# A bound on the experts' gather and scatter, with padding rows numbered past it

## The reference

```python
experts = (g_idx * EXPERTS_PER_GROUP + e_i).astype(jnp.int32)   # two of each token
...
pad_tok = jnp.full((p_len,), t, jnp.int32).at[dest].set(slot_tok[order])
pad_w = jnp.zeros((p_len,), jnp.float32).at[dest].set(slot_w[order])
...
hdn = jax.nn.silu(xb @ w1[e]) * (xb @ w3[e])
return hdn @ w2[e]
...
out = jnp.zeros((t + 1, dm), ys.dtype).at[pad_tok].add(ys * pad_w[:, None].astype(ys.dtype))
```

## Time and profile before

| | |
|---|---|
| median of three runs | 3437.43 us (3431.68 to 3441.14) |
| profiled execution, its own time | 3431.25 us |
| its span | 3429.7 us |
| mean granted TensorE clock | 0.932 of 2.4 GHz |
| PE, PEld, DVE, ACT, POOL busy | 84, 65, 45, 36, 9% of the span |
| DMA moved | 529.85 MB, mean 154 GB/s |
| the experts' phase | from about 1041 us to 1673 us |

### The profile page before, as it was taken

The page is one execution under the profiler, slowest core; times in us unless marked ns, Lnnn a source line. Parts: engine busy times, 40 slices in busy tenths (PEclk is TensorE's granted clock), DMA queues, the critical chain, the costliest instruction groups (busy, mean ns, idle before and its releaser), DMA issues. The chain is left out here.

```text
span 3429.7 us, 61238 instructions
## 1 busy us (share of the span) xinstructions
PE 2895.4 (84%) x22510; PEld 2246.3 (65%) x22510; DVE 1540.9 (45%) x2906; ACT 1219.3 (36%) x2193; POOL 301.7 (9%) x461
## 2 busy tenths in 40 slices
PE   7997885787977999999587999878887999868876
PEld 6785664565746887777476888744476888754455
DVE  3861666776251222222335411268744421068853
ACT  4332554566131000000333222268723222158831
POOL 0001641000021222221100000000000000000000
PEclk9998898898998999999798999979988999989988
DMA  5114553211358999999645221431054221251034
GB/s 184 68 70 145 142 151 99 72 35 44 115 189 309 375 379 380 379 376 378 234 132 172 90 103 49 135 119 38 10 175 163 95 98 73 98 172 31 14 123 166
DMA packets 241534, 529.85 MB, mean 154 GB/s; under 512 B 27760, under 2 KB 110640, under 8 KB 216720
## 3 DMA queue, kind: packets, MB, share of 16 engines
q1 hardware_dynamic: 216192, 464.40, 37.7%
q0 software_dynamic: 24080, 63.77, 6.6%
q10 hardware_dynamic: 1152, 0.27, 0.0%
HBM read 425.15 MB, written 104.15 MB: 154 GB/s over the span
## 5 line engine op out<-in xcount | busy, mean ns | idle before, releaser
L461 PE MATMUL ps<-in_wh,in_xh 128*128 (+1 forms) x1024 | 401.2, 392 | 0.0
L462 PE MATMUL ps<-in_wl,in_xh 128*128 (+1 forms) x1024 | 399.8, 390 | 0.0
L463 PE MATMUL ps<-in_wh,in_xl 128*128 (+1 forms) x1024 | 399.6, 390 | 0.0
L463 PEld LDWEIGHTS ps<-in_wh,in_xl 128*128 128x128 f32 x1024 | 193.0, 189 | 40.6
L461 PEld LDWEIGHTS ps<-in_wh,in_xh 128*128 128x128 f32 x1024 | 193.2, 189 | 39.7
L462 PEld LDWEIGHTS ps<-in_wl,in_xh 128*128 128x128 f32 x1024 | 193.1, 189 | 39.6
L1060 DVE TENSOR_TENSOR ex_hid<-ps,ex_act 32x128 f32<-32x128 f32 x96 | 28.2, 294 | 311.1 <-PE ps L1111 310.3
L461 PE MATMUL ps<-mix_in_wh,mix_in_xh 128*128 (+1 forms) x384 | 151.9, 396 | 9.0 <-DVE mix_in_out L381 5.5
L462 PE MATMUL ps<-mix_in_wl,mix_in_xh 128*128 (+1 forms) x384 | 149.9, 390 | 0.0
L463 PE MATMUL ps<-mix_in_wh,mix_in_xl 128*128 (+1 forms) x384 | 149.7, 390 | 0.0
L245 ACT COPY in_out<-ps 128x512 f32<-128x512 f32 x64 | 37.5, 587 | 248.7 <-PE ps L463 248.7
(11 more groups left out here) (412 smaller groups left out, 7281.2 us busy)
## 6 DMA issues: line engine op xcount, KB each, us to landing
ex_w_w1a<-in_w_dram SPq DMA_DIRECT2D x32, 1024.0 KB, 14.6
ex_w_w1b<-in_w_dram SPq DMA_DIRECT2D x32, 1024.0 KB, 15.6
ex_w_w3a<-in_w_dram SPq DMA_DIRECT2D x32, 1024.0 KB
ex_w_w3b<-in_w_dram SPq DMA_DIRECT2D x32, 1024.0 KB, 15.5
ex_w_w2a<-in_w_dram SPq DMA_DIRECT2D x32, 1024.0 KB, 15.6
ex_w_w2b<-in_w_dram SPq DMA_DIRECT2D x32, 1024.0 KB, 15.6
proj<-in_out SPq DMA_DIRECT2D x128, 256.0 KB, 2.0
da_w_ada<-in_w_ada_dram SPq DMA_DIRECT2D x32, 768.0 KB, 4.2
```

The costliest lines, as they stand in the source:

```text
L461: pe.matmul(o, xh[:, kt, tok], wb[0], start=(kt == 0), stop=False)
L462: pe.matmul(o, xh[:, kt, tok], wb[1], start=False, stop=False)
L463: last = pe.matmul(o, xl[:, kt, tok], wb[0], start=False, stop=(kt == KT - 1))
```

## The change

Both indirect transfers get an upper bound of 1023 on the index (`bounds_check=SEQ - 1`), and an index above it is not an error (`oob_is_err=False`). The padding triples name row 1024 to gather instead of row 0; their rows to add into were 1024 to 1151 before and stay so. So all indices of padding rows are above the bound, and the transfers are told to leave these rows out. Since rows of `xg` that are never gathered into would hold what memory held, POOL fills `xg` with zeros once, after the first index and row lists are asked for and before the first gather, and waits for that (`cleared`).

```diff
@@ expert_phase
-        copied = s.sem("copied")
+        copied, cleared = s.sem("copied"), s.sem("cleared")
...
                 pool.indirect_dma_start(out=xg[:], out_offset=None, in_=k.xn[:, :],
-                                        in_offset=bass.IndirectOffsetOnAxis(ap=idx_own[:, 0:1], axis=0)).then_inc(gathered, 16)
+                                        in_offset=bass.IndirectOffsetOnAxis(ap=idx_own[:, 0:1], axis=0), bounds_check=SEQ - 1, oob_is_err=False).then_inc(gathered, 16)
...
                 pool.indirect_dma_start(out=h[:, :], out_offset=bass.IndirectOffsetOnAxis(ap=row_own[:, 1:2], axis=0),
-                                        in_=y[:], in_offset=None, compute_op=ALU.add).then_inc(stored, 16)
+                                        in_=y[:], in_offset=None, compute_op=ALU.add, bounds_check=SEQ - 1, oob_is_err=False).then_inc(stored, 16)
...
             load_idx(0)
             load_row(0)
+            pool.memset(xg[:], 0.0).then_inc(cleared, 1)
+            pool.wait_ge(cleared, 1)
             gather(0)
@@ shape_constants
-    spares = np.stack([np.zeros(spare, int), SEQ + np.arange(spare) % P, np.zeros(spare, int)], 1).reshape(P, SPARE, 3)
+    spares = np.stack([np.full(spare, SEQ), SEQ + np.arange(spare) % P, np.zeros(spare, int)], 1).reshape(P, SPARE, 3)
```

## The result

| | before | after |
|---|---|---|
| median of 20 runs | 3435.43 us | 3439.09 us |
| lowest and highest | 3427.59 to 3441.14 | 3431.95 to 3446.31 |
| ratio, 95% interval | | **1.0015** (1.0008 to 1.0022) |
| span of the profiled execution | 3429.7 us | 3444.8 us |

The change is a loss of 0.15%, 5 us by the ratio. It is inside the bound of 0.3% that the prediction calls no change, but twenty runs each tell it from nothing, and it has the other sign than the 1.6 us of gain that was forecast.

What follows compares the result with a forecast made beforehand. DMA engines were taken to bound the expert phase, PE next. Profiled 3431.25 - 1.6 us (last gather), other terms zero, gave 3429.7 us, or 3436 us from the timed median 3437.43; own range 3428 to 3444, 8 in 10 3408 to 3444.

Steps and rivals of the forecast that it cites:

- The bound: Expert phase: DMA engines limit first, PE next; faster DMA can give about 1.2 us of the 18.4 us block.
- How a transfer is laid on the engines: Gather and scatter: 96 rows lie six consecutive per engine, so dropping the last rows leaves engine 0 its six.
- Step 1: Gather and scatter: 2144 padding rows not moved; worth 0 to 1.09 us per block, lower end taken.
- the 33rd gather: Last gather, all padding: leaves every engine, saving half of one block's q0 work, 1.6 us.
- The packets: POOL's queue q0: dropped rows leave no packets, so near 21900 packets after the change.
- Step 2: POOL's descriptor making: the compare on each index lies beside PE, hidden by slack; zero.
- Step 3: POOL's one memset of `xg`: 0.88 us, hidden in the 4.19 us wait for the index list; zero.
- Signs in the profile: Expert phase: period stays 18.4 us, `w1b` wait near 0.8 us per block, share 1.02 to 0.96, rate near 364 GB/s.
- A: Gather and scatter: rows dealt evenly over engines or a shared limit; 25 us faster, 3412 us; chance 0.22.
- B: Gather and scatter: the bound does not drop packets, rows clamped or moved anyway; 3437 us; chance 0.08.
- C: POOL's descriptor making: slow compare makes the scatter the bound; 16 us slower, 3453 us; chance 0.06.
- the 0.04 for the unforeseen: Whole kernel: chance 0.04 for what was not thought of, split between faster and slower.

Runs made afterwards that it cites:

- the even run: Kernel before, with bounds and the gather and scatter indices of two in every six rows raised above them, 32 rows per block dropped: 3403.74 us, ratio 0.9909.
- nothing scattered: Kernel before, with bounds and all 96 scatter indices of each block raised above theirs, the gather's inside: 3404.54 us, ratio 0.9911.
- the last 32 rows of each block: Kernel before, with bounds and the gather and scatter indices of partitions 64 to 95 raised above them: 3443.48 us, ratio 1.0030.
- the scatter alone: The change's bound on the scatter only, padding still gathering row 0, against the kernel before: 3448.57 us, ratio 1.0044.
- the gather alone: The change's bound on the gather only, the scatter's padding rows moved as before, against the kernel before: 3438.97 us, ratio 1.0012.
- the run with the bound idle: The change with padding numbers inside the bound (gather row 0, scatter bound 1151), so every row moves, against the kernel before: 3434.28 us, ratio 1.0005.
- once the padding was dealt: The change with each block's slots spread over the engines in the router, against the kernel before: 3415.36 us (0.9945); with one operation fewer per list 3411.35 us (0.9933).
- the four uneven runs: Against the kernel before: the change 1.0015, its bound on gather only 1.0012, on scatter only 1.0044, and partitions 64 to 95 dropped 1.0030.
- the pairs built for it: Kernel before moving only 64 rows, plus an additional load per block on sixteen, then ten partitions: 1.0489 and 1.0421 (28 KB pieces), 1.0433 and 1.0350 (8 KB).
- the 8 KB runs: Kernel before moving only 64 rows, plus three 8 KB pieces per partition and block on sixteen, then ten partitions: 3581.56 and 3555.45 us.

## Why the prediction was wrong, point by point

**The bound.** Right: DMA first, PE close behind. The estimate that faster DMA can give at most 1.2 us a block before PE binds held: 18.39 - 17.49 = 0.90 us in the even run and 0.97 with nothing scattered, with PE busy all of the time in both. One reading of the rows was loose: the two queues' 18.9 us a block are not the period of 18.4. They are 102.2% of it, since packets overlap, and 500 us hold 27.2 periods and not 27.

**How a transfer is laid on the engines.** Right for the index lists: the trace of before has 864 packets of 72 bytes in the 500 us, six triples of 12 bytes each, 32 a block. Six consecutive rows to an engine fits gather and scatter too: dropping two rows of every six gained 0.9 us a block, dropping the last 32 gained nothing, and with row i on engine i mod 16 both would have taken two rows from every engine. The rule of the Trainium skill named in the prediction (DMA: Bandwidth & Descriptors, "Why a DMA increments its semaphore by 16 and not by 1") agrees with it as to the 16 shares: a third fewer rows paid only where every share of six became smaller.

**Step 1, rows not moved: the step that failed.** The prediction took as its lower end "nothing, if the most loaded engine keeps all its rows", and then 1.6 us of gain for the 33rd gather. Zero was not the lower end. Uneven dropping costs: 5 us in the change, 10 us with the last 32 rows of each block, 15 us with the scatter alone, 4 us with the gather alone. The term measured +5 us, not -1.6. What the runs showed in its place: q1's packets took 4.3% longer (0.307 against 0.294 us), 3.7 points of share against the 5.8 that q0 gave up, and the rest went to engines that stood idle, so that the period grew by 0.12 us. An end of a range that is a resource's "no relief" is not a bound below when the same change can slow the others. Whether the 33rd gather gave anything can't be told beside this. Its price, half of a block's q0 work, was not measured by any run: q0's share changes with what runs beside it.

**The packets.** Wrong: near 21900 packets were expected on q0, and 24080 stood there. A dropped row is a small packet. It did not matter for the time where the rows were spread.

**Step 2, the compare.** Right to leave it at nothing: 951 to 1029 ns for the gather, 1490 and 1489 for the scatter, and 1.0005 for the run with the bound idle. **Step 3, the fill**: 0.97 us for 0.88, covered.

**Signs in the profile.** The period was to stay at 18.4 and came to 18.51, within the 0.3 us; the rate was to fall to 364 GB/s and fell to 363; `w1b` was still waited for. But the share was to fall from 1.02 to 0.96 and fell to 1.00: the idle engines were there, 10.7% of the time, but q1's longer packets filled much of the room.

**The rivals.** A's mechanism is not in the change, but its price was good: 25 us off, against 19 to 23 measured once the padding was dealt. B was half true in the packets and false in the bytes. C did not happen: DVE's copy waits for PE 27 times of 27. The real loss was none of the three, and lay in the 0.04 for the unforeseen. That the time still fell into the stated range says little: a loss of 5 us is smaller than the spread of the runs from which that range was taken.

**What stays open** is why dropping rows on some engines lengthens the weights' packets on the whole. Shown is that it goes with uneven dropping (0.298 to 0.311 us in the four uneven runs; 0.292 to 0.298 where the dropped rows of both transfers were spread, so the two kinds touch at one end). Small packets in a row are an unlikely cause: with six of them on every engine, the weights' packets that meet no row took 0.318 us. In the uneven runs themselves they were not tried apart. Not shown is that engines that run ahead of each other are the cause: the pairs built for it failed, and the run with nothing scattered has long packets without imbalance.

## What to carry to other kernels

Here rows saved in one piece at the end of a tile saved no time (1.0015 and 1.0030), and the same number taken evenly did (0.9909): spread the padding over the groups of consecutive partitions that each engine serves, and only then drop it. Before giving such a saving a lower bound of zero, ask what the relieved engines will do to the rest. Read the shares of both queues together with their packet counts, and then PE's waits and the period: a rising time per packet goes with a loss in the uneven runs, but with none where nothing was scattered.

## What was not expected of the hardware

- An index above the bound leaves a packet under 512 bytes: 2144 more of them for 2144 dropped rows, at the same total of 241534. Spread evenly they cost nothing that these runs can tell (3403.74 against 3406.45 us without any).
- Moving fewer bytes unevenly was slower than moving them all: 1.0030 for a third fewer rows.
- A weights' packet of 8 KB that met a row of the gather took 0.440 us, one that met a row of the scatter 0.329, each in the run without the other.
- An additional load of ten or sixteen partitions per block, 240 to 448 KB, stretched the period from 17.5 to between 22.5 and 24.1 us and q1's time per packet to 0.35 us and more in the 8 KB runs.
